# A transformer and state-space block on one Trainium2 core: slab products read their moving operand's two halves in turns

## The reference

```python
for i in range(DEPTH):                      # DEPTH = 2
    h = rms_norm(x, norm_mix_g[i])
    x = x + (dsa_mixer(h, ...) if i % 2 == 0 else retention_mixer(h, ...))
    x = x + conv_ffn(rms_norm(x, norm_ffn_g[i]), ...)   # D_FF = 2816
h = rmsnorm(x, norm_mix_w) * (1 + scale_m) + shift_m
x = x + gate_m * hybrid_mixer(h, ...)       # state-space part, pooling, gates
h = rmsnorm(x, norm_mlp_w) * (1 + scale_f) + shift_f
x = x + gate_f * (square(relu(h @ w_up)) @ w_down)      # D_FF_2 = 4096
return rmsnorm(x, norm_final_w)
```

## Time and profile before

| | us |
|---|---|
| median of 3 runs | 1186.0 |
| lowest, highest | 1185.4, 1186.12 |
| the profiled execution: its time | 1183.83 |
| its span, first to last instruction | 1182.0 |

### The profile page before, as it was taken

One profiled execution on the slowest core, in us unless ns is written; L12 is line 12 of the kernel. 1 busy time (PEld: TensorE's weight loads), 2 busy tenths in 40 slices (PEclk: granted clock), 3 DMA queues, 4 the chain that ended last, 5 costly groups with the idle time before them and its releaser, 6 DMA issues.

```text
span 1182.0 us, 25632 instructions
## 1 busy us (share of the span) xinstructions
PE 1163.4 (98%) x9126; PEld 1114.5 (94%) x9126; DVE 977.1 (83%) x1781; ACT 709.8 (60%) x1109; POOL 34.7 (3%) x64
## 2 busy tenths in 40 slices
PE   9999999999999999999999999999999999999997
PEld 7989999999899999999999999999999899999996
DVE  7877999888998898889888799999996667665666
ACT  6567656556546456556555577888866456544453
POOL 0000000000100010000000000000000000000000
PEclk9999999999999999999999999999999999999999
DMA  7535676664766786756665437457545556655551
GB/s 281 179 112 179 209 236 233 225 222 153 243 233 229 274 287 234 261 190 237 220 207 191 166 109 249 144 189 190 171 159 198 186 187 213 198 190 182 193 179 36
DMA packets 73041, 235.73 MB, mean 199 GB/s; under 512 B 7424, under 2 KB 16640, under 8 KB 72848
## 3 DMA queue, kind: packets, MB, share of 16 engines
q1 hardware_dynamic: 64304, 203.86, 51.6%
q0 software_dynamic: 8528, 30.98, 7.6%
q10 hardware_dynamic: 144, 0.02, 0.0%
HBM read 233.73 MB, written 1.09 MB: 199 GB/s over the span
## 4 chain that ended last, share of the span: by engine, by line
PE 82%; DVE 11%; issue 4%; ACT 3%; DVEq 1%; ACTq 0%
PE ps L202 25%; PE ps L203 24%; PE ps L204 24%; PE ps L234 3%; DVE w_lo L194 3%; PE ps L235 2%; DVE arena L1962 2%; ACT w_hi L189 1%; DVE arena L892 1%; DVE arena L1950 1%; PE ps L1627 0%; DVE arena L927 0%; DVE arena L1944 0%; DVE arena L455 0%; DVE arena L924 0%
## 5 line engine op out<-in xcount | busy, mean ns | idle before, releaser
L202 PE MATMUL ps<-a_hi,w_hi 128*128 128x256 f32 x1656 | 469.4, 283 | 2.4 <-DVE w_lo L194 1.6
L194 DVE TENSOR_TENSOR w_lo<-w_raw,w_hi 128x1024 fp32r<-128x1024 f32 x381 | 461.1, 1218 | 10.7 <-ACT w_hi L189 4.9
L203 PE MATMUL ps<-a_lo,w_hi 128*128 128x256 f32 x1656 | 462.5, 279 | 0.0
L204 PE MATMUL ps<-a_hi,w_lo 128*128 128x256 f32 x1656 | 462.3, 279 | 0.0
L189 ACT ACTIVATE w_hi<-w_raw 128x1024 fp32r<-128x1024 f32 x381 | 390.7, 1048 | 23.0 <-PE ps L204 12.5
L202 PEld LDWEIGHTS ps<-a_hi,w_hi 128*128 128x128 f32 x1656 | 311.4, 188 | 8.3 <-issue 4.6
L203 PEld LDWEIGHTS ps<-a_lo,w_hi 128*128 128x128 f32 x1656 | 311.5, 188 | 0.7 <-issue 0.2
L204 PEld LDWEIGHTS ps<-a_hi,w_lo 128*128 128x128 f32 x1656 | 311.4, 188 | 0.0
L202 PE MATMUL ps<-b_both,w_hi 128*128 128x256 f32 x560 | 158.1, 282 | 1.7 <-DVE b_both L952 0.9
L204 PE MATMUL ps<-b_both,w_lo 128*128 128x256 f32 x560 | 156.3, 279 | 0.0
L203 PE MATMUL ps<-b_both,w_hi 128*128 128x256 f32 x560 | 156.3, 279 | 0.0
(11 more groups left out here) (315 smaller groups left out, 1681.9 us busy)
## 6 DMA issues: line engine op xcount, KB each, us to landing
w_raw<-stream SPq DMA_DIRECT2D x381, 512.0 KB, 3.9
arena<-ada POOLq DMA_DIRECT2D x48, 512.0 KB, 6.0
c_both<-cum_rows POOLq DMA_DIRECT2D x4, 1024.0 KB
arena<-x SPq DMA_DIRECT2D x2, 512.0 KB, 4.4
con<-consts SPq DMA_DIRECT2D x1, 1024.0 KB, 5.7
arena<-row_cols POOLq DMA_DIRECT2D x2, 512.0 KB
arena<-c_rows POOLq DMA_DIRECT2D x1, 512.0 KB, 4.1
out<-arena SPq DMA_DIRECT2D x2, 256.0 KB, 2.2
```

What stands on the lines that cost most here:

```text
L194: dve.tensor_tensor(w_lo[:, s % RING], w_raw[:, s % RING], w_hi[:, s % RING].bitcast(F32), ALU.subtract).then_inc(w_lo_ready, 1)
L202: pe.matmul(o, wh, xh, start=start, stop=False, skip_group_check=shared)
L203: pe.matmul(o, wh, xl, start=False, stop=False, skip_group_check=shared)
L204: return pe.matmul(o, wl, xh, start=False, stop=stop, skip_group_check=shared)
```

## The change

The core of the diff, products first:

```diff
-                mm = mm3(pe, o, w_hi[:, s % RING, t], w_lo[:, s % RING, t], hi[:, k], lo[:, k],
+                mm = mm3(pe, by_two(o), w_hi[:, s % RING, t], w_lo[:, s % RING, t], woven(hi[:, k]), woven(lo[:, k]),
...
-                pe.matmul(ps[:, bank, :].rearrange("p (i t) -> p i t", i=2), w_hi[:, s % RING, t], both[:, k], start=first and k == 0, stop=False)
-                mm = pe.matmul(ps[:, bank, 0:SEQ], w_lo[:, s % RING, t], both[:, k, 0], start=False, stop=last and k == NT - 1)
+                pe.matmul(ps[:, bank, :].rearrange("p (i t a) -> p i t a", i=2, a=2), w_hi[:, s % RING, t],
+                          both[:, k].rearrange("p i (a t) -> p i t a", a=2), start=first and k == 0, stop=False)
+                mm = pe.matmul(by_two(ps[:, bank, 0:SEQ]), w_lo[:, s % RING, t], woven(both[:, k, 0]), start=False, stop=last and k == NT - 1)
...
-                return mm3(pe, down_sums(b, c0, c1), b_hi[:, o, t], b_lo[:, o, t], w_hi[:, s % RING, w], w_lo[:, s % RING, w],
+                return mm3(pe, crossed(down_sums(b, c0, c1)), b_hi[:, o, t], b_lo[:, o, t], cross(w_hi[:, s % RING, w]), cross(w_lo[:, s % RING, w]),
```

`two_slabs`, `down_slab`, the pooling products and the retention's values change in the same way, and `up_tile` gets a loop of its own with the plain read. The operands, on ScalarE and VectorE:

```diff
-            act.activation(a_hi[:, m], res[:, m], ACT.Copy, scale=pcol(g, m)).then_inc(a_hi_ready, 1)
+            act.activation(halves(a_hi[:, m]), parted(res[:, m]), ACT.Copy, scale=pcol(g, m)).then_inc(a_hi_ready, 1)
...
-                dve.tensor_tensor(glu[:, p % 2], gate[:, p % 2], conv[:, p % 2, 1], ALU.mult).then_inc(f["glu"], 1)
+                dve.tensor_tensor(halves(glu[:, p % 2]), parted(gate[:, p % 2]), parted(conv[:, p % 2, 1]), ALU.mult).then_inc(f["glu"], 1)
...
-                        ins = dve.tensor_tensor(turn_t[:, n], ps[:, bank + x_h, 0:SEQ], table, ALU.mult)
+                        ins = dve.tensor_tensor(halves(turn_t[:, n]), parted(ps[:, bank + x_h, 0:SEQ]), halves(table), ALU.mult)
...
-                dve.tensor_tensor(c_lo[:, 2 * g:2 * g + 2], win_of(g), c_hi[:, 2 * g:2 * g + 2].bitcast(F32), ALU.subtract).then_inc(pooled_operand, 1)
+                for m in (2 * g, 2 * g + 1):
+                    ins = dve.tensor_tensor(halves(c_lo[:, m]), parted(win_of(g)[:, m % 2]), halves(c_hi[:, m].bitcast(F32)), ALU.subtract)
+                ins.then_inc(pooled_operand, 1)
```

More of the change, by code:

```diff
@@ L67, with parted, halves, woven @@
     CONSTS += _w
+def parted(x):
+    return x.rearrange("p (t a) -> p a t", a=2)
+def halves(x):
+    return x.rearrange("p (a t) -> p a t", a=2)
+def woven(x):
+    return x.rearrange("p (a t) -> p t a", a=2)
+def by_two(x):
+    return x.rearrange("p (t a) -> p t a", a=2)
+def cross(x):
+    return x.rearrange("p (c a t) -> p c t a", a=2, t=P)
+def crossed(x):
+    return x.rearrange("p (c t a) -> p c t a", a=2, t=P)
+def uncross(x):
+    return x.rearrange("p (c t a) -> p c a t", a=2, t=P)
+def plain(x):
+    return x.rearrange("p (c a t) -> p c a t", a=2, t=P)
 def val(base, it=None, step=0):
@@ L224, in two_slabs @@
                     n = (s + i) % RING
-                    mm = mm3(pe, o, w_hi[:, n, t], w_lo[:, n, t], hi[:, k], lo[:, k], k == 0, k == NT - 1)
+                    mm = mm3(pe, by_two(o), w_hi[:, n, t], w_lo[:, n, t], woven(hi[:, k]), woven(lo[:, k]), k == 0, k == NT - 1)
                     if k == NT - 1:
@@ L243, in down_slab @@
                 o = ps[:, m // 2, (m % 2) * SEQ:(m % 2 + 1) * SEQ]
-                mm = mm3(pe, o, w_hi[:, s % RING, t], w_lo[:, s % RING, t], hi, lo,
+                mm = mm3(pe, by_two(o), w_hi[:, s % RING, t], w_lo[:, s % RING, t], woven(hi), woven(lo),
                          first and m % 2 == 0, last, shared=True)
@@ L387, in vec_prep @@
             dve.wait_ge(a_hi_ready, NT * v + m + 1)
[L388 removed]
+            dve.scalar_tensor_tensor(out=halves(a_lo[:, m]), in0=(halves if v == 2 else parted)(res[:, m]), scalar=pcol(g, m), in1=halves(a_hi[:, m].bitcast(F32)),
                                      op0=ALU.mult, op1=ALU.subtract).then_inc(a_ready, 1)
@@ L1411, in head @@
                     dve.wait_ge(g_silu, per_head(e + 1, 4, h, it))
-                    dve.tensor_tensor(y_b[:, e], y_n[:, e % 2], g_b[:, e], ALU.mult).then_inc(y_ready, 1)
+                    dve.tensor_tensor(halves(y_b[:, e]), parted(y_n[:, e % 2]), parted(g_b[:, e]), ALU.mult).then_inc(y_ready, 1)
                     if e:
@@ L1466, in low @@
                 dve.wait_ge(a_hi_ready, NT * 4 + m + 1)
-                dve.scalar_tensor_tensor(out=a_lo[:, m], in0=gained[:, m], scalar=mix_shift(m), in1=a_hi[:, m].bitcast(F32),
+                dve.scalar_tensor_tensor(out=halves(a_lo[:, m]), in0=parted(gained[:, m]), scalar=mix_shift(m), in1=halves(a_hi[:, m].bitcast(F32)),
                                          op0=ALU.add, op1=ALU.subtract).then_inc(a_ready, 1)
@@ L1922, in tail @@
                     for t in range(4):
-                        ins = dve.scalar_tensor_tensor(out=y_f[:, t], in0=z_s[:, t], scalar=prm(34 + t, g, it), in1=inv_s,
+                        ins = dve.scalar_tensor_tensor(out=halves(y_f[:, t]), in0=parted(z_s[:, t]), scalar=prm(34 + t, g, it), in1=parted(inv_s),
                                                        op0=ALU.mult, op1=ALU.mult)
@@ L2076, in merge_tile @@
                 dve.wait_ge(parts_gated, val(m + 1, it, 2))
-                dve.tensor_tensor(merged[:, u], part[:, u, 0], part[:, u, 1], ALU.add).then_inc(merged_ready, 1)
+                dve.tensor_tensor(halves(merged[:, u]), parted(part[:, u, 0]), parted(part[:, u, 1]), ALU.add).then_inc(merged_ready, 1)
                 dve.wait_ge(merged_hi, val(m + 1, it, 2))
@@ L2140, in up_tile @@
             def up_tile(n, it=None, each=None):
-                slab_gemm(pe, up_at(n), ps[:, 4 + n % 3, 0:SEQ + 2], c_hi_wide, c_lo_wide, it, 6, each=each)
+                s = up_at(n)
+                slab_ready(pe, s, it, 6)
+                for k in range(NT):
+                    if each:
+                        each(k)
+                    t = slice(k * P, (k + 1) * P)
+                    mm = mm3(pe, ps[:, 4 + n % 3, 0:SEQ + 2], w_hi[:, s % RING, t], w_lo[:, s % RING, t], c_hi_wide[:, k], c_lo_wide[:, k],
+                             k == 0, k == NT - 1)
+                mm.then_inc(w_used, 1)
             def down_piece(n, b, c0, c1):
```

31 lines of the change are left out of this document (16 added, 15 removed).

## The result

The changed kernel takes 1154.9 us (median of 6, 1153.5 to 1155.55), the kernel before 1185.68 (1183.89 to 1186.12, 6 runs on the same chip): a ratio of 0.9743, interval 0.9733 to 0.9753, so 30.8 us or 2.6% less. The forecast was 1147 with a range of 1120 to 1194: 38 to 39 us of gain were forecast.

The account below looks back on a forecast made before the run. TensorE was taken as the bound, its products paying 8% extra for the moving read. Saving 72 us, cut to 50 by VectorE's limits, less 12 for layout, gave 38: 1186 - 38 = 1148, stated as 1147, range 1120 to 1194.

Parts of the forecast that it names:

- The 8%: All TensorE products: 0.45 ns a column against 0.417 for one clock period, an excess put down to the moving read.
- The first rival: Read in turns is slower: 256-column steps over 117 ns; at 0.87 ns a column about 2,080 us; chance 0.16.
- 8.6 ns for each 256-column product: Saving per changed 256-column product at 0.417 ns a column; 7080 of them give 61 us of the 72.
- the third rival: The stationary load floors 256-column steps at 112 ns, saving 4.7 each; whole kernel 1162 us; chance 0.14.
- VectorE's limits, 72 down to 50: Per stage, the smaller of TensorE's saving and VectorE's waits for TensorE, attention halved; 72 us becomes 50.
- the cap of 1.9: Stage from 660 to 885 us: TensorE's saving of 13.8 limited to VectorE's waits for TensorE, 1.9 us.
- VectorE has slack: Stage from 885 to 1000 us, with `both_slab`: TensorE's saving of 7.9 us counted whole.
- The layout, 12 us: Stepped reads in 140 VectorE operations cost 0 to 37 us; a third, 12, taken, so 50 becomes 38.
- The fourth rival: VectorE takes the gain back: 262 ns for each stepped operation leaves 13 us, 1173 us; chance 0.10.
- The granted clock stays at 1.00: Sign for the profile after: TensorE's granted clock unchanged at 1.00, the 2.4 GHz level.
- The other signs: VectorE's L204 waits nearly gone from 121 to 660, L202 waits for `w_lo`, `up_tile` unchanged, `product`, turns, `y_b` 420 to 690 ns.
- the halved attention: Stage from 0 to 121 us: half of TensorE's 5.8 us taken, 3, as products stand between top-k and softmax steps.

Follow-up runs that it names:

- experiment 3: Changed kernel with operands written in the new layout, even tokens first, but every product reading in plain order: 1184.36 us, ratio 0.9996.
- experiment 1: A separate kernel of nothing but blocks of 24 products, each block with one form of read, computing nothing of the reference; 512 columns: plain 226.7 ns, in turns 215.8.
- experiments 7 and 8: State-space convolution taps on VectorE cut to their first columns: 7 in the kernel before, 1181.53 us (0.9969); 8 in the changed kernel, 1146.85 us (0.9673).
- experiment 2: Changed kernel with reads in turns kept but tiles written in the old plain order: 1151.75 us, ratio 0.9721.
- experiments 4 and 5: 4: changed kernel plus four unread products in TensorE's wait for the softmax, 1153.42 us (0.9735); 5: changed kernel again, unaltered, 1154.83 us (0.9743).

## Why the prediction was right, and where it was off

- **The 8% are the read of the moving operand, and turns take them away.** Right. The steps changed where the read was changed, stayed at 119.2 in `up_tile`, and experiment 3 with the new layout and the old read has the time of the kernel before. The first rival, a slower read, did not come; experiment 1 shows how near it stood: four parts instead of two cost 283 ns, runs of two 339. The rule of the Trainium skill that the prediction weighed ("SBUF — State Buffer", Door 1: at least two accesses in a row must hit a line of 16 bytes) would have made the read in turns slower. The measurement goes against it for two places, 215.8 ns against 226.7. It also goes against it for runs of two (339) and for a step of two elements (451), which have two accesses to each line and are slow; for a step of four (460), which has one, the rule and the measurement agree.
- **8.6 ns for each 256-column product.** This is the step that was mis-sized: 5.1 came. The 512-column products met their forecast (215 to 217 forecast, 215.9 measured). The 256-column ones stop at the load's floor of 111.7, which is the third rival's mechanism with nearly the price that the rival gave (4.7). So by the prediction's own sign, a step of 112, the third rival came true, and the term 7080 x 8.6 = 61 is 7080 x 5.1 = 36. The measured time doesn't tell the two apart: 1154.9 lies 8 us above the forecast of 1147 and 7 below the rival's 1162. That it is near the forecast is luck. The prediction held the very row in its hand, the float32 step of 112, used it as proof that the array has no excess, and gave the other reading 0.14. That one row can't tell the two apart. Other rows of the kernel before could have: eight plain float32 products of a single moving column, each with a load of 128, and the product behind them:

```profile
60.71 0.95 PE L560 MATMUL ps<-con,sq 128*128 128x1 f32 x8
61.52 0.37 PE L202 MATMUL ps<-a_hi,w_hi 128*128 128x256 f32 x1
```

0.81 us for eight, 0.10 us each with next to nothing to stream: a cost of the product that doesn't shrink with its columns.

- **VectorE's limits, 72 down to 50.** The method held in the main: with the right steps the same sum gives 1.7 + 7.8 + 6.5 + 1.9 + 7.6 + 1.9 + 5.9 + 5.9 = 39, against 28.7 between the spans and 30.8 between the medians. The feed-forward and output stages came within 1.4 us of it. In the state-space stage 0.9 came of a possible 5.6, and experiments 7 and 8 show that most of the rest was VectorE's. But the cap of 1.9 there was near by luck: it is what L1112 (`evict`) waits, which belongs to the second feed-forward part, whose end falls into that window. From 695 to 852 us VectorE waits 0.5 for TensorE, so the method itself gives 0.5. Too high were attention (1.7 against -1.7), retention (6.5 against 3.9; L1404 and the slab split of VectorE stand in the chain there) and the merge (5.9 against 3.8), where "VectorE has slack" was true of its mean and not of the slab splits that TensorE waits 2.3 us for. In these three no experiment took VectorE's work away; in attention and retention it is argued that it is VectorE.
- **The layout, 12 us.** Too high: 29 to 39 ns an operation from SBUF, none from PSUM, 2.6 us in the difference between experiment 2 and the change. This covered a part of the first miss: 39 - 3 = 36 stands where 50 - 12 = 38 stood. The fourth rival (262 ns each) was far off.
- **"The granted clock stays at 1.00."** Wrong: the wait that grows was followed by a fall in every profile without the idle products, which goes with 0.6 to 2.2 us more of attention (experiments 4 and 5). That the longer wait is the cause isn't shown, as the kernel before had a fall in one profile of two (experiment 7). Most of the negative gain in the table is of that one profile: in the other one of the changed kernel attention ended at 100.33, 0.5 behind the kernel before.
- **The other signs.** VectorE's waits in the feed-forward parts fell to 7.2 us of 20.5, TensorE's waits for `w_lo` rose from 2.0 to 5.3 us, and `up_tile` kept its step. The turns stayed at 415 ns, a little under the range given for them.

So the sum was near for a reason that is not all its own: the largest term was too high by 25 us; VectorE's caps and the halved attention took up 14 of these, so that the sum falls only from 50 to 39; and a layout that cost 9 less than feared stood against 9 of the remaining 11. That leaves 36, and 5 more are missing, most of them in attention, retention and merge.

## What to carry to other kernels

For 4-byte moving operands, reading exactly two places at least 4 elements apart in turns brings a 512-column product from 227 to 216 ns and a 256-column one from 117 to 119 down to 112; other patterns made it slower, so measure the one you mean by itself. Before you price a cheaper instruction, look for a second cost of the same instruction that doesn't shrink with it (here the load of 128 columns for each product), and treat the shortest such step in the trace as the bound until something shorter is seen. Where two engines are within a few per cent of each other, take from the faster one no more than the other now waits for it, and check each wait that will grow for what it does to the clock. Look in the trace for products with very few moving columns: they show what a product costs apart from its columns.

## What was not expected of the hardware

- The distance of the two places doesn't matter from 4 to 256 elements (all 215.8 ns), and 2 apart is as slow as plain (228 against 226.7).
- A plain 512-column product takes 226.7 ns alone and 233 in the kernel, where slabs are written and moved beside it; in turns it takes 215.8 and 215.9: the read in turns doesn't show what goes on beside it. What the 6 ns are is open, all the more as the plain 256-column product is the other way round, 119.6 alone and 116.7 in the kernel.
- A 512-column product that starts at an odd element takes (142.53 - 136.84) / 24 = 237 ns plain (L114 and L116 of experiment 1's timeline), 216.7 in turns.
- A product of 64 columns is no cheaper than one of 256 (110.8 and 111.7 ns), and using the same stationary tile again saves nothing.
- Reading the stationary tile with a step of four elements brings a 128-column product from 111.3 to 234 ns, with a step of two only to 115.8.
- A wait of 2.5 us before a stretch of short products was followed by a clock of 0.60 to 0.72 over the next 5 us in four profiles of four; one of 1.64 us by 0.77 in one profile of three, and four idle products in the wait kept it at 1.00 in two of two.
- VectorE pays about 30 ns for a step of two in 256 elements of SBUF, and nothing for it in PSUM (415 ns both times).
